# Splitting a weight tile in one pass of 1024 columns or in two of 512, on ScalarE and VectorE

## The chip, the core and the metric

The kernel runs on one core of a Trainium2 chip. The metric is the device time of one execution in microseconds (us); lower is better. Its engines are TensorE (PE in the profile; PEld is its weight load), VectorE (DVE), ScalarE (ACT), GpSimd (POOL) and SyncE (SP), which issues the weight transfers.

## What is computed

Two layers of a decoder trunk on 256 tokens of 1024 channels, all in float32. Cut to what matters here:

```python
def reference(x, ...):
    for l in range(2):
        h = rms_norm(x, norm_mix_g[l])
        mix = conv_sgu_mixer(h, ...) if l % 2 == 0 else moba_mixer(h, ...)
        x = x + mix
        h = rms_norm(x, norm_ffn_g[l])
        x = x + peer(h, peer_w_q[l], peer_subkeys[l], peer_u[l], peer_v[l])
    return rms_norm(x, norm_final_g)

def peer(h, w_q, subkeys, u_tab, v_tab):     # 128^2 one-neuron experts, 8 heads, 16 experts each
    q = (h @ w_q).reshape(T, 8, 2, 128)
    s = einsum('thpd,hpkd->thpk', q, subkeys)
    ...                                       # top 16 of each side, then top 16 of their sums
    act = gelu(einsum('td,thkd->thk', x, u_tab[expert]))
    return einsum('thk,thkd->td', softmax(sc) * act, v_tab[expert])
```

The kernel does not gather experts: it multiplies with the whole tables `u` and `v` (each 16384 x 1024) and uses gates that are zero where an expert was not picked.

## The kernel before

**Tiles and split.** All weights are streamed as 600 tiles of 128 partitions x 1024 columns: `w_in` 16, `w_out` 8, `q0` 16, `u0` 128, `v0` 128, `qkv` 24, `w_o` 8, `q1` 16, `u1` 128, `v1` 128 (table `STREAM`). SyncE loads each tile into one of 4 buffers `raw`. A float32 product is made of three matmuls in the type fp32r, so each tile is split into a high and a low part: ScalarE rounds it (`w_hi`, line 406), and VectorE subtracts the rounded value from the raw one (`w_lo`, line 603). The activations are split in the same way (`x_hi`, `x_lo`, or `ag_hi`, `ag_lo` for the table `v`). TensorE then runs 24 matmuls of 128x256 for each tile: 8 blocks `m` of 128 columns, times high by high, high by low, low by high (lines 1035 to 1037 in `project`, 1180 to 1182 in `combine`).

**Halves.** The split is made in halves of 512 columns. `w_hi` and `w_lo` have 4 buffers of one half each, which is two tiles. The semaphore `hi_ready` counts rounded halves, `split_ready` subtracted halves (TensorE waits for it ahead of each half, SyncE for the second half of the tile that is to be overwritten), `half_used` counts halves that TensorE has finished.

**Order.** There is no scheduler: the order on each engine is the order in which the code stands, and waits are on semaphores. All engines work two tiles ahead. On ScalarE (`taking`) one step is: wait until tile n is used, take its result out of PSUM (`take`), then round both halves of tile n+2 (`ahead`). For `w_out` and `w_o`, ScalarE only rounds (`only_ahead`), and VectorE takes the result (`add_residual`). On VectorE the two subtractions of tile n+2 stand between the other work of that step:

- in the `q` stages (`q_body`), between the pieces that rank the scores of the keys (`rank_keys`);
- in the first 8 turns of each `u` stage (`u_body`, a turn is 4 tiles), one half ahead of each of the 8 pieces of `pick` (maxima, places, comparison line 812, masks line 819, sums line 824). These are called pick turns below;
- in turns 9 to 16 of `u` (`late_body`), behind two `one_hots`, whose result TensorE scatters with 16 small matmuls for each tile (line 1147); in the remaining turns (`early_body`) behind one `one_hots` and ahead of `gate_late` and `apply_gates`;
- in the `v` stages (`v_body`), behind the subtraction that makes `ag_lo` (line 967).

The conv, gating and attention parts between the projections have no weight tiles.

Of the kernel before, what the change touches and what calls it, by code (L numbers as in the profile page):

```python
# [20 lines left out]
F32 = mybir.dt.float32  # L21
# [7 lines left out]
P = 128  # L29
# [39 lines left out]
SPLIT = 4  # L69
# [61 lines left out]
def build(nc, a, out):  # L131
    ctx = ExitStack()
    with ctx:
# [12 lines left out]
        w_hi = sb("w_hi", [P, SPLIT, HALF], F32R)  # L146
        w_lo = sb("w_lo", [P, SPLIT, HALF], F32R)
# [93 lines left out]
        half_used = sem("half_used")  # L241
# [157 lines left out]
        def _(act):  # L399
            def round_half(name, k, j, b):  # L400

                u = 2 * (TILE0[name] + 4 * k + j) + b
                act.wait_ge(loaded[j % RAW], loaded_count(name, k, j))
                at_least(act, half_used, u - SPLIT + 1)
                s = (2 * j + b) % SPLIT
                act.activation(w_hi[:, s, :], raw[:, j % RAW, b * HALF:(b + 1) * HALF], ACT.Copy).then_inc(hi_ready, 1)  # L406

            def ahead(name, k, j):

                if isinstance(k, int) and TILE0[name] + 4 * k + j + 2 >= TILES:  # L410
                    return
                for b in range(2):
                    round_half(name, k, j + 2, b)

            def taking(name, take, turns, k0=0, first=0, last=0, besides=None):

                def body(k):
                    for j in range(4):
                        act.wait_ge(half_used, 2 * (TILE0[name] + 4 * (k + k0) + j) + 2)
# [28 lines left out]
            for j in range(2):  # L448
                for b in range(2):
                    round_half("w_in", 0, j, b)  # L450
# [44 lines left out]
            def experts(l):  # L495
# [48 lines left out]
                def body(k):  # L544
                    for j in range(4):
                        act.wait_ge(half_used, 2 * (TILE0[act_v] + 4 * k + j) + 2)
                        round_ag(k, j)
                        ahead(act_v, k, j)
                sweep(act, NKEYS // 4, body, last=1)

            def taking_first(name, take):
                def body(k):
                    for j in range(4):
                        act.wait_ge(half_used, 2 * (TILE0[name] + 4 * k + j) + 2)
# [42 lines left out]
        def _(dve):  # L597
            def lower_half(name, k, j, b):

                u = 2 * (TILE0[name] + 4 * k + j) + b  # L600
                dve.wait_ge(hi_ready, u + 1)
                s = (2 * j + b) % SPLIT
                dve.tensor_tensor(w_lo[:, s, :], raw[:, j % RAW, b * HALF:(b + 1) * HALF], w_hi[:, s, :].bitcast(F32),  # L603
                                  ALU.subtract).then_inc(split_ready, 1)

            def ahead(name, k, j, last_wait=None):

                if isinstance(k, int) and TILE0[name] + 4 * k + j + 2 >= TILES:
                    return
                for b in range(2):  # L610
                    if b and last_wait:
                        dve.wait_ge(*last_wait)
                    lower_half(name, k, j + 2, b)
# [44 lines left out]
            for j in range(2):  # L658
                for b in range(2):
                    lower_half("w_in", 0, j, b)  # L660
# [28 lines left out]
            def add_residual(name):  # L689
                def body(k):  # L690
                    for j in range(4):
                        dve.wait_ge(half_used, 2 * (TILE0[name] + 4 * k + j) + 2)
# [192 lines left out]
            def experts(l):  # L885
# [5 lines left out]
                def q_body(k):  # L891
                    for j in range(4):
# [7 lines left out]
                        lower_half(q, k, j + 2, 0)  # L900
# [3 lines left out]
                        lower_half(q, k, j + 2, 1)  # L904
# [73 lines left out]
                dve.wait_ge(half_used, 2 * (TILE0[v] + NKEYS))  # L978
# [42 lines left out]
        def _(pe):  # L1021
            def project(name, k, j, operand=None):
# [4 lines left out]
                for b in range(2):  # L1027
                    pe.wait_ge(split_ready, 2 * n + b + 1)
                    s = (2 * j + b) % SPLIT
                    for i in range(4):  # L1030
                        m = 4 * b + i
                        if operand is not None and isinstance(k, int) and k == j == 0 and m % 2 == 0:
                            pe.wait_ge(operand_ready[operand], m // 2 + 1)
                        hi, lo = (w[:, s, i * P:(i + 1) * P] for w in (w_hi, w_lo))
                        pe.matmul(proj_ps[j % 2], hi, x_hi[:, m, :], start=(m == 0), stop=False)  # L1035
                        pe.matmul(proj_ps[j % 2], hi, x_lo[:, m, :], start=False, stop=False)  # L1036
                        mm = pe.matmul(proj_ps[j % 2], lo, x_hi[:, m, :], start=False, stop=(m == KD - 1))  # L1037
                    mm.then_inc(half_used, 1)
# [75 lines left out]
            def experts(l):  # L1114
# [53 lines left out]
                def combine(k):  # L1168
                    for j in range(4):
# [3 lines left out]
                        for b in range(2):  # L1173
                            pe.wait_ge(split_ready, 2 * n + b + 1)
                            s = (2 * j + b) % SPLIT
                            for c in range(4):
                                m = 4 * b + c
                                hi, lo = (w[:, s, c * P:(c + 1) * P] for w in (w_hi, w_lo))

                                pe.matmul(y_ps[:, m, :], hi, ag_hi[:, j % 2, :], start=begin and m % 2 == 0, stop=False, skip_group_check=True)  # L1180
                                pe.matmul(y_ps[:, m, :], hi, ag_lo[:, j % 2, :], start=False, stop=False, skip_group_check=True)  # L1181
                                mm = pe.matmul(y_ps[:, m, :], lo, ag_hi[:, j % 2, :], start=False, stop=end, skip_group_check=True)  # L1182
                            mm.then_inc(half_used, 1)
# [94 lines left out]
```

## Time and profile before

| | |
|---|---|
| device time, median of 3 runs | 2322.8 us (2320.18 to 2323.11) |
| span of the profiled execution | 2329.5 us (no other time is kept for it) |
| TensorE busy | 2168.4 us, 93% |
| TensorE weight load busy | 2090.0 us, 90% |
| VectorE busy | 1646.3 us, 71% |
| ScalarE busy | 1037.1 us, 45% |
| DMA | 323.57 MB, 139 GB/s over the span |

By start and end in the profiled execution, the stages of layer 0 lie about here: `w_in` 30 to 77 us, conv and gating to 162, `w_out` to 186, `q0` 196 to 271, pick turns of `u0` 274 to 389, turns 9 to 16 to 553, the rest of `u0` to 790, `v0` to 1163; then `qkv`, attention, `w_o`, and layer 1's `q1`, `u1`, `v1` in the same form. Busy times are averages over stages with different limits, so a stage is read by its own rows. The engines' busy times overlap and are not to be added. A busy TensorE is read by the distance between the starts of its matmuls, since each matmul is drawn longer than that distance.

### The profile page before, as it was taken

Reading aid. Unit: us, or ns where it says so; the run is one execution under the profiler, and the core shown is the slowest. Engines: PE = TensorE matmul, PEld = TensorE weight load, DVE = VectorE, ACT = ScalarE, POOL = GpSimd, SP = SyncE. Lnnn points to the kernel's source line nnn. Section 1 sums busy time; section 2 is a strip of 40 time slices with the busy share of each in tenths; the row PEclk is TensorE's granted clock in tenths of the full one; section 3 lists DMA queues with packets and bytes.
Section 4 is the critical chain, followed back from the end, with each engine's and each line's share of the span. In section 5 each row is a group of like instructions: output and inputs, shape, how many; then the busy total and the mean of one; then the engine's idle time right before and its main releaser. Section 6 shows DMA issues by size and latency. Waiting matters only on the chain.

```text
span 2329.5 us, 52851 instructions
## 1 busy us (share of the span) xinstructions
PE 2168.4 (93%) x17092; PEld 2090.0 (90%) x17092; DVE 1646.3 (71%) x3922; ACT 1037.1 (45%) x2162; POOL 19.8 (1%) x43
## 2 busy tenths in 40 slices
PE   6778798999999999999999987989999999999998
PEld 5558788999999999999987677889999999999998
DVE  3657998777888655555544589977788886555555
ACT  4334355444333355555544443544443333555554
POOL 1000000000000000000001000000000000000000
PEclk9779999999999899999998999999999998999999
DMA  5203344333443355555552233433334343555553
GB/s 179 73 23 115 115 162 140 106 107 126 138 141 137 116 180 180 183 185 181 182 184 95 71 111 117 162 128 108 108 128 143 136 143 119 183 184 180 180 182 125
DMA packets 90032, 323.57 MB, mean 139 GB/s; under 512 B 9914, under 2 KB 11994, under 8 KB 89728
## 3 DMA queue, kind: packets, MB, share of 16 engines
q1 hardware_dynamic: 88528, 316.71, 39.8%
q0 software_dynamic: 1456, 6.23, 0.8%
q8 instruction: 29, 0.48, 0.1%
q14 instruction: 19, 0.16, 0.0%
HBM read 321.82 MB, written 1.08 MB: 139 GB/s over the span
## 4 chain that ended last, share of the span: by engine, by line
PE 75%; DVE 12%; issue 9%; ACT 2%; DVEq 1%; DMA 0%; POOL 0%; ACTq 0%; POOLq 0%
PE psum L1180 11%; PE psum L1181 11%; PE psum L1182 11%; PE psum L1035 10%; PE psum L1036 9%; PE psum L1037 9%; PE psum L1147 9%; DVE w_lo L603 2%; DVE big L812 1%; ACT w_hi L406 1%; PE psum L1205 1%; DVE big L824 1%; PE psum L1208 1%; DVE big L819 1%; PE psum L1047 1%
## 5 line engine op out<-in xcount | busy, mean ns | idle before, releaser
L603 DVE TENSOR_TENSOR w_lo<-raw,w_hi 128x512 fp32r<-128x512 f32 x1200 | 781.8, 687 | 245.4 <-ACT w_hi L406 242.5
L1035 PE MATMUL psum<-x_hi,w_hi 128*128 128x256 f32 x2752 | 808.9, 294 | 77.9 <-DVE w_lo L603 44.5
L1036 PE MATMUL psum<-x_lo,w_hi 128*128 128x256 f32 x2752 | 785.3, 285 | 0.0
L1037 PE MATMUL psum<-x_hi,w_lo 128*128 128x256 f32 x2752 | 785.2, 285 | 0.0
L406 ACT ACTIVATE w_hi<-raw 128x512 fp32r<-128x512 f32 x1200 | 685.6, 619 | 39.4 <-PE psum L1037 28.8
L1035 PEld LDWEIGHTS psum<-x_hi,w_hi 128*128 128x128 f32 x2752 | 534.8, 194 | 91.1 <-DVE w_lo L603 57.1
L1180 PE MATMUL psum<-ag_hi,w_hi 128*128 128x256 f32 x2048 | 581.9, 284 | 2.9 <-DVE ag_lo L967 2.9
L1181 PE MATMUL psum<-ag_lo,w_hi 128*128 128x256 f32 x2048 | 581.5, 284 | 0.0
L1182 PE MATMUL psum<-ag_hi,w_lo 128*128 128x256 f32 x2048 | 581.4, 284 | 0.0
L1036 PEld LDWEIGHTS psum<-x_lo,w_hi 128*128 128x128 f32 x2752 | 535.5, 195 | 0.0
L1037 PEld LDWEIGHTS psum<-x_hi,w_lo 128*128 128x128 f32 x2752 | 534.1, 194 | 0.0
L1180 PEld LDWEIGHTS psum<-ag_hi,w_hi 128*128 128x128 f32 x2048 | 395.2, 193 | 3.3 <-DVE ag_lo L967 3.3
L1181 PEld LDWEIGHTS psum<-ag_lo,w_hi 128*128 128x128 f32 x2048 | 395.3, 193 | 0.0
L1182 PEld LDWEIGHTS psum<-ag_hi,w_lo 128*128 128x128 f32 x2048 | 395.3, 193 | 0.0
L967 DVE TENSOR_TENSOR ag_lo<-big,ag_hi 128x256 fp32r<-128x256 f32 x256 | 108.8, 425 | 307.2 <-ACT ag_hi L537 306.3
L1147 PE MATMUL psum<-hot_i,hot_j 128*128 128x68 f32 (+1 forms) x2048 | 262.7, 277 | 12.4 <-DVE big L876 5.4
L1147 PEld LDWEIGHTS psum<-hot_i,hot_j 128*128 128x128 f32 x2048 | 253.7, 197 | 18.8 <-DVE hot_i L870 10.6
L537 ACT ACTIVATE ag_hi<-big 128x256 fp32r (+1 forms) x252 | 105.2, 417 | 366.4 <-PE psum L1182 366.4
L867 DVE TENSOR_TENSOR hot_j<-const,picks 128x512 f32<-128x512 f32 x256 | 174.8, 683 | 0.0
L528 ACT ACTIVATE fresh<-psum 128x256 f32<-128x256 f32 x120 | 46.1, 384 | 279.8 <-PE psum L1037 279.8
L507 ACT ACTIVATE big<-psum 128x256 f32 x136 | 52.1, 383 | 209.7 <-PE psum L1037 209.3
L865 DVE TENSOR_TENSOR hot_i<-const,picks 128x240 f32<-128x240 f32 (+1 forms) x256 | 106.7, 417 | 1.4 <-PE psum L1147 0.7
(149 smaller groups left out, 1156.5 us busy)
## 6 DMA issues: line engine op xcount, KB each, us to landing
raw<-in_peer_u SPq DMA_DIRECT2D x256, 512.0 KB, 3.2
raw<-in_peer_v SPq DMA_DIRECT2D x256, 512.0 KB, 3.4
raw<-in_peer_q SPq DMA_DIRECT2D x32, 512.0 KB, 3.3
raw<-in_w_qkv SPq DMA_DIRECT2D x24, 512.0 KB, 3.2
raw<-in_w_in SPq DMA_DIRECT2D x16, 512.0 KB, 3.5
raw<-in_w_out SPq DMA_DIRECT2D x8, 512.0 KB, 3.3
raw<-in_w_o SPq DMA_DIRECT2D x8, 512.0 KB, 3.3
big<-bias_scratch POOLq DMA_DIRECT2D x1, 3072.0 KB, 12.1
```

The lines of the kernel that those rows point to most:

```text
L406: act.activation(w_hi[:, s, :], raw[:, j % RAW, b * HALF:(b + 1) * HALF], ACT.Copy).then_inc(hi_ready, 1)
L603: dve.tensor_tensor(w_lo[:, s, :], raw[:, j % RAW, b * HALF:(b + 1) * HALF], w_hi[:, s, :].bitcast(F32), ALU.subtract).then_inc(split_read ...
L865: dve.tensor_tensor(own_i, numbers[:, :, i0:i0 + rows].to_broadcast([P, 4, rows]), ahead_of[0].to_broadcast([P, 4, rows]), ALU.is_equal).t ...
L867: dve.tensor_tensor(own_j, numbers.to_broadcast([P, 4, P]), ahead_of[1].to_broadcast([P, 4, P]), ALU.is_equal).then_inc(hot_step, 1)
L967: dve.tensor_tensor(ag_lo[:, j % 2, :], big[:, bass.ds(i * T, T)], ag_hi[:, j % 2, :].bitcast(F32), ALU.subtract).then_inc(ag_ready, 1)
L1035: pe.matmul(proj_ps[j % 2], hi, x_hi[:, m, :], start=(m == 0), stop=False)
L1036: pe.matmul(proj_ps[j % 2], hi, x_lo[:, m, :], start=False, stop=False)
L1037: mm = pe.matmul(proj_ps[j % 2], lo, x_hi[:, m, :], start=False, stop=(m == KD - 1))
L1147: mm = pe.matmul(misc_ps[half][:, i * rows:(i + 1) * rows], hot_j[:, 4 * half + i, :], hot_i[:, 4 * half + i, 0:rows], start=True, stop=True)
L1180: pe.matmul(y_ps[:, m, :], hi, ag_hi[:, j % 2, :], start=begin and m % 2 == 0, stop=False, skip_group_check=True)
L1181: pe.matmul(y_ps[:, m, :], hi, ag_lo[:, j % 2, :], start=False, stop=False, skip_group_check=True)
L1182: mm = pe.matmul(y_ps[:, m, :], lo, ag_hi[:, j % 2, :], start=False, stop=end, skip_group_check=True)
```

## The change

Each tile is rounded by one ScalarE operation of 1024 columns and subtracted by one VectorE operation of 1024 columns. `w_hi` and `w_lo` have two buffers of a whole tile, so the memory is the same. `hi_ready`, `split_ready` and the renamed `tile_used` count tiles. TensorE waits once per tile, ahead of its first matmul. On VectorE, the subtraction stands where the first half stood (in `q_body` where the second stood), and the pieces that had a half between them follow each other.

```diff
-SPLIT = 4
+SPLIT = 2
...
-        w_hi = sb("w_hi", [P, SPLIT, HALF], F32R)
-        w_lo = sb("w_lo", [P, SPLIT, HALF], F32R)
+        w_hi = sb("w_hi", [P, SPLIT, D], F32R)
+        w_lo = sb("w_lo", [P, SPLIT, D], F32R)
...
-                    at_least(sp, split_ready, 2 * (TILE0[name] + 4 * k + j - RAW) + 2)
+                    at_least(sp, split_ready, TILE0[name] + 4 * k + j - RAW + 1)
...
-            def round_half(name, k, j, b):
-
-                u = 2 * (TILE0[name] + 4 * k + j) + b
+            def round_tile(name, k, j):
+
+                n = TILE0[name] + 4 * k + j
                 act.wait_ge(loaded[j % RAW], loaded_count(name, k, j))
-                at_least(act, half_used, u - SPLIT + 1)
-                s = (2 * j + b) % SPLIT
-                act.activation(w_hi[:, s, :], raw[:, j % RAW, b * HALF:(b + 1) * HALF], ACT.Copy).then_inc(hi_ready, 1)
+                at_least(act, tile_used, n - SPLIT + 1)
+                act.activation(w_hi[:, j % SPLIT, :], raw[:, j % RAW, :], ACT.Copy).then_inc(hi_ready, 1)
...
-            def lower_half(name, k, j, b):
-
-                u = 2 * (TILE0[name] + 4 * k + j) + b
-                dve.wait_ge(hi_ready, u + 1)
-                s = (2 * j + b) % SPLIT
-                dve.tensor_tensor(w_lo[:, s, :], raw[:, j % RAW, b * HALF:(b + 1) * HALF], w_hi[:, s, :].bitcast(F32),
+            def lower_tile(name, k, j):
+
+                dve.wait_ge(hi_ready, TILE0[name] + 4 * k + j + 1)
+                s = j % SPLIT
+                dve.tensor_tensor(w_lo[:, s, :], raw[:, j % RAW, :], w_hi[:, s, :].bitcast(F32),
                                   ALU.subtract).then_inc(split_ready, 1)
...
                         new[0]()
-                        lower_half(q, k, j + 2, 0)
                         if old:
                             old[3]()
                         dve.wait_ge(scores_copied, 16 * l + r + 1)
-                        lower_half(q, k, j + 2, 1)
+                        lower_tile(q, k, j + 2)
                         new[1]()
...
-                        lower_half(u, k, i // 2 + 2, i % 2)
+                        if i % 2 == 0:
+                            lower_tile(u, k, i // 2 + 2)
                         parts[i]()
...
-                for b in range(2):
-                    pe.wait_ge(split_ready, 2 * n + b + 1)
-                    s = (2 * j + b) % SPLIT
-                    for i in range(4):
-                        m = 4 * b + i
+                pe.wait_ge(split_ready, n + 1)
+                s = j % SPLIT
+                for m in range(KD):
...
-                    mm.then_inc(half_used, 1)
+                mm.then_inc(tile_used, 1)
```

Two places show what this does to the order. The first is VectorE in a pick turn, from the end of the piece `second_places` to the comparison (`big` holds all scratch tiles, `pick_step` is VectorE's own counter of these pieces). Before:

```order
L801 MAX_INDEX big<-big 128x8 x2
L769 ISA
L769 COPY big<-big 128x100
L601 ISA
L603 TENSOR_TENSOR w_lo<-raw,w_hi 128x512 [waits hi_ready]
L806 REGISTER_ALU
L807 CAST big<-big 128x2x8 [waits pick_step]
L601 REGISTER_ALU
L603 TENSOR_TENSOR w_lo<-raw,w_hi 128x512 [waits hi_ready]
L810 REGISTER_ALU
L812 TENSOR_TENSOR big<-big,const 128x800 [waits pick_step]
L812 TENSOR_TENSOR big<-big,const 128x800
```

With the change:

```order
L793 MAX_INDEX big<-big 128x8 x2
L761 ISA
L761 COPY big<-big 128x100
L597 REGISTER_ALU
L599 TENSOR_TENSOR w_lo<-raw,w_hi 128x1024 [waits hi_ready]
L798 REGISTER_ALU
L799 CAST big<-big 128x2x8 [waits pick_step]
L802 REGISTER_ALU
L804 TENSOR_TENSOR big<-big,const 128x800 [waits pick_step]
L804 TENSOR_TENSOR big<-big,const 128x800
```

The half that stood between the conversion (CAST) and the comparison is gone, so the comparison waits for the conversion directly in front of it. The other three tiles of a turn change in the same way.

The second place is VectorE in the loop of a `v` stage, one step of it and the start of the next. Before:

```order
L967 TENSOR_TENSOR ag_lo<-big,ag_hi 128x256
L601 ISA
L603 TENSOR_TENSOR w_lo<-raw,w_hi 128x512 [waits hi_ready]
L601 REGISTER_ALU
L603 TENSOR_TENSOR w_lo<-raw,w_hi 128x512 [waits hi_ready]
L966 REGISTER_ALU
L967 ISA [waits ag_hi_ready]
L967 TENSOR_TENSOR ag_lo<-big,ag_hi 128x256
```

With the change:

```order
L959 TENSOR_TENSOR ag_lo<-big,ag_hi 128x256
L597 REGISTER_ALU
L599 TENSOR_TENSOR w_lo<-raw,w_hi 128x1024 [waits hi_ready]
L958 REGISTER_ALU
L959 ISA [waits ag_hi_ready]
L959 TENSOR_TENSOR ag_lo<-big,ag_hi 128x256
```

Where the first of two subtractions could start behind the first rounded half, the one subtraction starts behind the whole rounded tile.

## Rows read from the trace of the kernel before

**Rows 1.** The page: its first line, and the chain that ended last by engine

```profile
span 2329.5 us, 52851 instructions
...
PE 75%; DVE 12%; issue 9%; ACT 2%; DVEq 1%; DMA 0%; POOL 0%; ACTq 0%; POOLq 0%
```

**Rows 2.** Windows, pick turns and v0: stretch, length, busy (instructions) PE PEld DVE ACT POOL, clock, DMA

```profile
290.00:389.00 99.00, 90.23 (x720) 87.19 (x720) 90.01 (x251) 52.41 (x100) 0.00 (x0) 1.00 0.48 162
...
800.00:1160.00 360.00, 360.00 (x3002) 360.00 (x3002) 212.70 (x376) 182.02 (x375) 0.00 (x0) 1.00 0.53 182
```

**Rows 3.** Groups of instructions: busy us, mean ns of one, then idle before

```profile
L603 DVE TENSOR_TENSOR w_lo<-raw,w_hi 128x512 fp32r<-128x512 f32 x1200 | 781.8, 687 | 245.4 <-ACT w_hi L406 242.5 <-DVE big L824 1.9 <-DVE big L769 0.2
L406 ACT ACTIVATE w_hi<-raw 128x512 fp32r<-128x512 f32 x1200 | 685.6, 619 | 39.4 <-PE psum L1037 28.8 <-DMA raw<-in_w_in 7.5 <-PE psum L1182 3.1
...
L460 ACT ACTIVATE big<-big 128x1024 f32<-128x1024 f32 x2 | 2.0, 1048 | 0.0
...
L649 DVE TENSOR_TENSOR big<-big 128x1024 f32<-128x1024 f32 x2 | 2.5, 1225 | 0.1
```

**Rows 4.** Timeline of v0, one step: start us, length us, engine, line

```profile
902.58 1.14 ACT L406 ACTIVATE w_hi<-raw 128x512 fp32r<-128x512 f32 x2
...
903.23 1.29 DVE L603 TENSOR_TENSOR w_lo<-raw,w_hi 128x512 fp32r<-128x512 f32 x2
...
904.83 0.28 PE L1180 MATMUL psum<-ag_hi,w_hi 128*128 128x256 f32 x1
...
905.14 0.42 ACT L537 ACTIVATE ag_hi<-big 128x256 fp32r x1 [1.42 <-PE psum L1182]
```

**Rows 5.** Timeline of VectorE, one pick turn of u0

```profile
316.06 0.69 DVE L603 TENSOR_TENSOR w_lo<-raw,w_hi 128x512 fp32r<-128x512 f32 x1 [0.16 <-DVE big L824]
...
321.03 0.69 DVE L603 TENSOR_TENSOR w_lo<-raw,w_hi 128x512 fp32r<-128x512 f32 x1 [0.59 <-ACT w_hi L406]
...
322.32 1.89 DVE L812 TENSOR_TENSOR big<-big,const 128x800 f32<-128x800 f32 x2
...
329.16 0.69 DVE L603 TENSOR_TENSOR w_lo<-raw,w_hi 128x512 fp32r<-128x512 f32 x1 [0.16 <-DVE big L824]
```

**Rows 6.** Timeline of ScalarE in the same turn

```profile
320.09 0.38 ACT L507 ACTIVATE big<-psum 128x256 f32 x1 [2.66 <-PE psum L1037]
320.37 1.14 ACT L406 ACTIVATE w_hi<-raw 128x512 fp32r<-128x512 f32 x2
```

**Rows 7.** Timeline of TensorE in the same turn, behind a wait

```profile
316.81 0.39 PE L1035 MATMUL psum<-x_hi,w_hi 128*128 128x256 f32 x1 [0.94 <-DVE w_lo L603]
317.03 0.28 PE L1036 MATMUL psum<-x_lo,w_hi 128*128 128x256 f32 x1
```

**Rows 8.** Timeline of turns 9 to 16 of u0, one tile: three engines

```profile
458.52 1.14 ACT L406 ACTIVATE w_hi<-raw 128x512 fp32r<-128x512 f32 x2
...
459.18 1.29 DVE L603 TENSOR_TENSOR w_lo<-raw,w_hi 128x512 fp32r<-128x512 f32 x2 [2.17 <-ACT w_hi L406]
...
461.77 2.34 PE L1147 MATMUL psum<-hot_i,hot_j 128*128 128x60 f32 x16 [0.28 <-DVE hot_i L870]
```

**Rows 9.** Timeline of VectorE in q0: the first half of two successive tiles

```profile
225.32 0.68 DVE L603 TENSOR_TENSOR w_lo<-raw,w_hi 128x512 fp32r<-128x512 f32 x1
...
229.50 0.68 DVE L603 TENSOR_TENSOR w_lo<-raw,w_hi 128x512 fp32r<-128x512 f32 x1
```

**Rows 10.** Timeline of w_in, one tile

```profile
50.86 1.29 DVE L603 TENSOR_TENSOR w_lo<-raw,w_hi 128x512 fp32r<-128x512 f32 x2 [1.59 <-ACT w_hi L406]
...
50.21 1.15 ACT L406 ACTIVATE w_hi<-raw 128x512 fp32r<-128x512 f32 x2
```

**Rows 11.** Timeline of VectorE, the first pick turn of u0

```profile
281.75 0.69 DVE L603 TENSOR_TENSOR w_lo<-raw,w_hi 128x512 fp32r<-128x512 f32 x1 [2.69 <-ACT w_hi L406]
```

**Rows 12.** Timelines of w_out (ScalarE) and of the last turns of u0 (VectorE)

```profile
167.97 0.63 ACT L406 ACTIVATE w_hi<-raw 128x512 fp32r<-128x512 f32 x1 [0.81 <-PE psum L1037]
...
607.34 1.29 DVE L603 TENSOR_TENSOR w_lo<-raw,w_hi 128x512 fp32r<-128x512 f32 x2 [0.56 <-ACT w_hi L406]
```

More of the change, by code:

```diff
@@ L240, in build @@
         split_ready = sem("split_ready")
-        half_used = sem("half_used")
+        tile_used = sem("tile_used")
         proj_taken = sem("proj_taken")
@@ L448, in _ @@
             for j in range(2):
-                for b in range(2):
-                    round_half("w_in", 0, j, b)
+                round_tile("w_in", 0, j)
             act.wait_ge(line_ps, 1)
@@ L597, in _, with ahead @@
         def _(dve):
-            def lower_half(name, k, j, b):
-                u = 2 * (TILE0[name] + 4 * k + j) + b
-                dve.wait_ge(hi_ready, u + 1)
-                s = (2 * j + b) % SPLIT
-                dve.tensor_tensor(w_lo[:, s, :], raw[:, j % RAW, b * HALF:(b + 1) * HALF], w_hi[:, s, :].bitcast(F32),
+            def lower_tile(name, k, j):
+                dve.wait_ge(hi_ready, TILE0[name] + 4 * k + j + 1)
+                s = j % SPLIT
+                dve.tensor_tensor(w_lo[:, s, :], raw[:, j % RAW, :], w_hi[:, s, :].bitcast(F32),
                                   ALU.subtract).then_inc(split_ready, 1)
-            def ahead(name, k, j, last_wait=None):
+            def ahead(name, k, j):
                 if isinstance(k, int) and TILE0[name] + 4 * k + j + 2 >= TILES:
                     return
[L610 to L613, printed above, removed]
+                lower_tile(name, k, j + 2)
             def norm(r, gain, s):
@@ L658, in _ @@
             for j in range(2):
-                for b in range(2):
-                    lower_half("w_in", 0, j, b)
+                lower_tile("w_in", 0, j)
             dve.wait_ge(params_in, 16 * PARAMS)
@@ L977, in experts @@
                 sweep(dve, NKEYS // 4, v_body, last=1)
-                dve.wait_ge(half_used, 2 * (TILE0[v] + NKEYS))
+                dve.wait_ge(tile_used, TILE0[v] + NKEYS)
                 for m in range(KD):
@@ L1026, in project @@
                 at_least(pe, proj_taken, p - 1)
-                for b in range(2):
-                    pe.wait_ge(split_ready, 2 * n + b + 1)
-                    s = (2 * j + b) % SPLIT
-                    for i in range(4):
-                        m = 4 * b + i
[L1032 to L1037, printed above, removed]
-                    mm.then_inc(half_used, 1)
+                pe.wait_ge(split_ready, n + 1)
+                s = j % SPLIT
+                for m in range(KD):
+                    if operand is not None and isinstance(k, int) and k == j == 0 and m % 2 == 0:
+                        pe.wait_ge(operand_ready[operand], m // 2 + 1)
+                    hi, lo = (w[:, s, m * P:(m + 1) * P] for w in (w_hi, w_lo))
+                    pe.matmul(proj_ps[j % 2], hi, x_hi[:, m, :], start=(m == 0), stop=False)
+                    pe.matmul(proj_ps[j % 2], hi, x_lo[:, m, :], start=False, stop=False)
+                    mm = pe.matmul(proj_ps[j % 2], lo, x_hi[:, m, :], start=False, stop=(m == KD - 1))
+                mm.then_inc(tile_used, 1)
             def projections(name, tiles, operand=None):
@@ L1172, in combine @@
                         begin, end = isinstance(i, int) and i == 0, isinstance(i, int) and i == NKEYS - 1
[L1173 to L1183, printed above, removed]
+                        pe.wait_ge(split_ready, n + 1)
+                        s = j % SPLIT
+                        for m in range(KD):
+                            hi, lo = (w[:, s, m * P:(m + 1) * P] for w in (w_hi, w_lo))
+                            pe.matmul(y_ps[:, m, :], hi, ag_hi[:, j % 2, :], start=begin and m % 2 == 0, stop=False, skip_group_check=True)
+                            pe.matmul(y_ps[:, m, :], hi, ag_lo[:, j % 2, :], start=False, stop=False, skip_group_check=True)
+                            mm = pe.matmul(y_ps[:, m, :], lo, ag_hi[:, j % 2, :], start=False, stop=end, skip_group_check=True)
+                        mm.then_inc(tile_used, 1)
                 sweep(pe, NKEYS // 4, combine, first=1, last=1)
```

10 lines of the change are left out of this document (5 added, 5 removed).

## The prediction

> **What bounds the kernel now.** I read the chain of waits first: TensorE holds 75% of it and VectorE 12% [rows 1], so most of the span is matmuls back to back, and VectorE sets the pace in a few stages. The windows say which. In a `v` stage TensorE is busy all of 360 us at full clock, with VectorE at 59% and ScalarE at 51% [rows 2]; one tile takes 2.88 us (ScalarE's step recurs at that distance, and the 24 matmuls start 0.12 apart). In the pick turns both engines are near their limit: TensorE 91%, VectorE 91% [rows 2], and a turn of 4 tiles takes 329.16 - 316.06 = 13.10 us [rows 5], against 4 x 2.88 = 11.52 of matmuls. In the `q` stages VectorE has no gap and a tile takes 229.50 - 225.32 = 4.18 us [rows 9].
>
> So what counts is not the busy time of the split but its **latency**: TensorE finishes tile n, ScalarE takes the result and rounds tile n+2, VectorE subtracts, and TensorE needs the result 2.88 us later, when tile n+1 is done. With halves this chain is a short pipeline: VectorE works on the first half while ScalarE rounds the second, and TensorE starts with the first. The change makes the three run one after the other.
>
> **Prices of the two new operations.** Two roundings of 512 last 1.14 us together [rows 4], 0.52 from start to start and 0.62 for the last. For one of 1024 the nearest row is another ScalarE operation of that shape: 1.05 us [rows 3]. From 0.62 for 512, with 0.42 for the 512 columns more, it would be 1.04; I take 1.04 (bounds 1.00 and 1.06). Two subtractions last 1.29 [rows 4], 0.60 and 0.69. One of 1024 is 1.225 by the nearest row [rows 3]; I take 1.22 (bounds 1.20 and 1.24), of which the next operation overlaps 0.08, as it does now (0.69 against 0.60). So VectorE saves 2 x 0.60 - 1.14 = 0.06 us for each tile, and ScalarE 0.10.
>
> ScalarE: Activation LUTs, in the section on what a table load costs, of the Trainium skill prices an operation without pointer operands at 186 ns + 0.833 ns per column, with 93 ns of overlap between neighbours. That gives 613 ns for 512 columns, which the rows bear out, and 1039 for 1024; by it the sum would be the same.
>
> **`v` stages (256 tiles).** Rounding starts at 902.58 [rows 4] and would end at 903.62. VectorE starts 0.04 behind it (in `w_in` the first rounded half, 50.21 + 0.61 = 50.82, is followed at 50.86 [rows 10]): 903.66 to 904.88. TensorE starts 0.06 behind a subtraction it waits for (316.06 + 0.69 = 316.75, then 316.81 [rows 5, 7]): 904.94. Now it starts that tile at 904.83 [rows 4], so it is 0.11 late; and behind a wait the second matmul follows at 0.22 instead of 0.12 [rows 7], another 0.10. This 0.21 comes back once for every two tiles, since the loop runs over tile n and n+2 (one loop for the even tiles, one for the odd, and the delay of one shifts the other): 0.105 us per tile, 256 x 0.105 = **+27**. Bounds: without the 0.10 it is 14; with the upper prices (0.04 more) 32.
>
> **`w_in`, `qkv`, and the last 4 plain tiles of each pick stage (48 tiles).** The same loop; only the taking in front is 0.28 instead of 0.32 long, so 0.17 per two tiles: 48 x 0.085 = **+4** (0 to 5). In `w_out` and `w_o` ScalarE rounds without taking anything: it could start at 167.97 [rows 12], the chain ends at 167.97 + 1.04 + 0.04 + 1.22 + 0.06 = 170.33, and that tile is due near 170.5 (one tile after its neighbour, which begins about 0.3 ahead of 167.97). I cost it at nothing; if the cover is gone, 16 tiles by 0.1 are 2 us.
>
> **Pick turns (8 per layer, 16).** The turn runs round a loop: first subtraction, TensorE's tile, ScalarE's taking and rounding, third subtraction, comparison, masks, sums, first subtraction of the next turn. Now the third subtraction starts 321.03 - 316.06 = 4.97 behind the first and has waited 0.59 for ScalarE [rows 5]. With the change: subtraction 1.22, TensorE 0.06, to the taking 320.09 - 316.81 = 3.28 [rows 6, 7], to the rounding 0.28, rounding 1.04, VectorE 0.04, which is 5.92; with TensorE's 0.10 behind a wait, 6.02. That is **+1.05**, and VectorE idles for some 1.5 us there, because its own pieces ahead are shorter by two halves. Then third subtraction to comparison: now 1.29 [rows 5]; after, 1.14 + 0.17 for the conversion + about 0.14 for the wait on it, which no filler covers any more (such a wait shows as 0.16 [rows 5]): 1.45, **+0.16**. From there to the next turn 6.84 [rows 5] loses 0.06. Sum +1.15 per turn, 16 turns: **+18** (without the bare wait and the 0.10: 14; with two more bare waits: 22). Each pick stage also ends with a tile that TensorE gets whole instead of by halves: 1.22 - 0.69 = 0.5, twice: **+1**.
>
> **Turns 9 to 16 of `u` (8 per layer).** Only one tile of each turn is tight: a table load of 1.28 us stands ahead of ScalarE's taking, and TensorE then waits 0.28 for `one_hots` [rows 8], which stand behind the subtraction on VectorE. The next operation there comes at 458.52 + 1.04 + 0.04 + 1.14 = 460.74 instead of 459.18 + 1.21 = 460.39: 0.35 later, and TensorE with it: 16 x 0.35 = **+6** (4 to 7). The other three tiles have no table load in the chain, 1.28 us more room; in the last turns of `u` VectorE sits idle 0.56 us per tile [rows 12], more than the 0.35: 0.
>
> **`q` stages.** VectorE is full, so 30 tiles by 0.06: **-2**. The copy of the scores is then followed by `second_values`, whose inputs are an operation older; I cost it at nothing (3 if each paid 0.1).
>
> SyncE's load into a raw buffer is released by the subtraction, 0.4 us later than now; the buffer is wanted again four tiles on, about 9 us, and the transfer takes 3.4: nothing. GpSimd has no part in this.
>
> **Sum**: 27 + 4 + 18 + 1 + 6 - 2 = +54 us. It is made against the profiled execution, whose span of 2329.5 [rows 1] lies 0.3% above the median of 2322.8; I put it on the median: 2377.
>
> **Rivals.**
>
> *The `v` loop is just not late.* The margin is 0.11 us in a chain of seven steps; if the subtraction took 1.11 or the rounding 0.93, all tiles outside the pick and late turns would be on time. Against it: both 1024-column rows. Time: 54 - 31 = +23, 2346.
>
> *The clock falls in the pick turns.* TensorE's wait at the head of a turn grows from 0.94 to about 2.1 us. In the first pick turn, which begins after 8.8 us of idle TensorE, VectorE waits 2.69 for ScalarE instead of 0.59 [rows 11], since the matmuls there run slower. If every turn paid these 2.1 us more: 16 x 2.1 = 34, 2411. Against it: the granted clock is 1.00 in these turns with gaps of 0.9 and 0.3 [rows 2, 7], and 2.1 is nearer to those than to 8.8.
>
> *Faster: fewer operations on a full engine.* The pick turns go by VectorE's work alone: it saves 4 x 0.06 per turn, and loses its 0.59 wait too, if the rounded tile is there when VectorE comes to the third subtraction. Then a turn takes 13.10 - 0.24 - 0.59 = 12.27, 16 turns save 13, the `q` stages 2, and the `v` loop holds: 2308. It decides whether ScalarE's rounding ends within 4.3 us (4.97 - 0.59 - 2 x 0.06) of the first subtraction's start; by my steps it ends at 6.0. For it speaks only the busy share of 91%; the 0.59 us wait on ScalarE speaks against. VectorE: DVE Perf Modes of the Trainium skill, rules for kernel authors, advises to keep the count of chained VectorE operations low rather than the count of semaphores; by that rule this rival would be the outcome, and the trace agrees with it only where VectorE never waits, in the `q` stages.
>
> That the change does not do what it says is excluded: the order shows one operation of 1024 on VectorE where two stood.
>
> **Chances.** Forecast (a loss in all three kinds of stage, 2358 to 2394 on its own) 0.77; `v` loop on time 0.09; clock 0.07; faster 0.05; all of it smaller than thought, within 0.2% (what a measurement of this kernel can tell from no change) 0.02. The range takes in the second case and the bounds: 2344 to 2398; outside are the clock and the two last cases. Faster 0.05, same 0.02, slower 0.93.
>
> **What would show it.** In `v`, TensorE should have a gap of about 0.1 us ahead of every tile or a double one ahead of every second, put down to the subtraction, and ScalarE's step should recur at 2.98 us. A pick turn should last 14.25 us, with about 1.5 us of waiting for ScalarE at the third subtraction. In turns 9 to 16 the wait of 0.28 should be 0.63. VectorE should be busy some 40 us less (600 tiles by 0.06). The prediction is wrong if the `v` stages keep 2.88 us a tile or the clock leaves 1.00.

## The result and the profile after

| | before | with the change |
|---|---|---|
| device time, median | 2322.95 us (2320.18 to 2324.05, 4 runs) | 2390.91 us (2385.75 to 2394.66, 4 runs) |
| span of the profiled execution | 2329.5 us | 2392.9 us (the run of 2394.66) |

The ratio is 1.0287, 95% interval 1.0262 to 1.0311: slower by 68 us. The forecast was 2377, with 2344 to 2398 as its range.

The page of the changed kernel, first line, busy lines and the chain that ended last, against [rows 1]:

```profile
span 2392.9 us, 49989 instructions
...
PE 2211.6 (92%) x17092; PEld 2110.7 (88%) x17092; DVE 1617.6 (68%) x3322; ACT 980.7 (41%) x1562; POOL 19.8 (1%) x43
...
PE 75%; DVE 11%; issue 10%; ACT 3%; DVEq 1%; DMA 0%; POOL 0%; ACTq 0%; POOLq 0%
```

VectorE worked 29 us less (some 40 were forecast) and ScalarE 56 us less, in 600 fewer operations each, and the kernel is 63 us longer by the spans. The page's groups of the two operations, against [rows 3]:

```profile
L599 DVE TENSOR_TENSOR w_lo<-raw,w_hi 128x1024 fp32r<-128x1024 f32 x600 | 734.5, 1224 | 407.9 <-ACT w_hi L405 405.0
...
L405 ACT ACTIVATE w_hi<-raw 128x1024 fp32r<-128x1024 f32 x600 | 628.8, 1048 | 44.6 <-PE psum L1027 33.6
```

One operation lasts 1.224 and 1.048 us, as forecast (1.22 and 1.04). What grew is VectorE's idle time ahead of the subtraction, nearly all of it waiting for ScalarE: 242.5 us before, 405.0 now.

Where the time went shows in the lengths of the stages, taken between the first starts of the operation that opens each (the scaling of `topi` for the pick stage, `picks`, the first `fresh`, the first `ag_hi`, the first addition of `y_ps`), in us:

| layer 0 / layer 1 | pick turns | turns 9 to 16 | rest of `u` | `v` |
|---|---|---|---|---|
| before | 123.1 / 122.7 | 160.0 / 161.1 | 234.5 / 234.4 | 374.2 / 371.6 |
| with the change | 133.4 / 134.4 | 168.4 / 166.5 | 235.1 / 235.1 | 386.9 / 383.8 |
| difference of both | +22.0 | +13.8 | +1.3 | +24.9 |

These make 62.0 of the 63.4 us.

One stretch changes its length from one run to the next, whatever the kernel, and has to be left out of comparisons: the attention of layer 1, from its first matmul with `anti` to the first addition of `w_o`. It took 69.3 us in the profile of before and 69.3 in that of the change, so these two compare fairly; in five of the eight experiments below it took 62. The window at its beginning, with the change (stretch, length, busy time of PE, PEld, DVE, ACT and POOL, each with its number of instructions, granted clock, DMA share, GB/s):

```profile
1285.00:1300.00 15.00, 14.74 (x31) 7.32 (x32) 4.21 (x10) 2.65 (x9) 2.23 (x7) 0.56 0.09 33
```

The same place in the profile of `act_whole`, a kernel of the next section:

```profile
1267.00:1282.00 15.00, 14.34 (x58) 7.92 (x58) 7.79 (x19) 5.41 (x19) 3.83 (x10) 1.00 0.09 33
```

So some 7 to 8 us between two runs of one kernel may be this alone. The unprofiled runs of before (2318 to 2324) have about the length that the short form would give: the profiled span of 2329.5 makes some 2331 of device time, if the 1.8 us between span and time of the change hold here too. That they have the short form was not seen. It may be one reason why the medians differ by 68 and the spans by 63.

The timeline of ScalarE and VectorE in `v0`, against [rows 4] (start us, length us):

```profile
940.47 0.42 ACT L534 ACTIVATE ag_hi<-big 128x256 fp32r x1 [1.52 <-PE psum L1170]
...
943.53 0.42 ACT L534 ACTIVATE ag_hi<-big 128x256 fp32r x1 [1.69 <-PE psum L1170]
943.85 1.04 ACT L405 ACTIVATE w_hi<-raw 128x1024 fp32r<-128x1024 f32 x1
...
944.93 1.23 DVE L599 TENSOR_TENSOR w_lo<-raw,w_hi 128x1024 fp32r<-128x1024 f32 x1 [0.42 <-ACT w_hi L405]
...
946.41 0.42 ACT L534 ACTIVATE ag_hi<-big 128x256 fp32r x1 [1.52 <-PE psum L1170]
```

The steps are 3.06 and 2.88 in turn: 5.94 for two tiles instead of 5.76. Rounding ends at 944.89, VectorE starts at 944.93 and ends at 946.16. TensorE's rows there:

```profile
946.00 0.28 PE L1170 MATMUL psum<-ag_hi,w_lo 128*128 128x256 f32 x1
946.21 0.38 PE L1168 MATMUL psum<-ag_hi,w_hi 128*128 128x256 f32 x1
946.43 0.28 PE L1169 MATMUL psum<-ag_lo,w_hi 128*128 128x256 f32 x1
```

It starts the tile 0.05 behind the end of the subtraction; the two distances of 0.21 and 0.22 replace two of 0.12, so the second matmul is 0.19 late. A stall this short hardly shows in the busy share, because the drawn end of one matmul covers it.

One pick turn on VectorE, against [rows 5]:

```profile
319.98 1.23 DVE L599 TENSOR_TENSOR w_lo<-raw,w_hi 128x1024 fp32r<-128x1024 f32 x1
...
325.89 1.23 DVE L599 TENSOR_TENSOR w_lo<-raw,w_hi 128x1024 fp32r<-128x1024 f32 x1 [1.16 <-ACT w_hi L405]
327.04 0.17 DVE L799 CAST big<-big 128x16 f32<-128x16 uint32 x1
327.24 1.90 DVE L804 TENSOR_TENSOR big<-big,const 128x800 f32<-128x800 f32 x2
...
334.00 1.23 DVE L599 TENSOR_TENSOR w_lo<-raw,w_hi 128x1024 fp32r<-128x1024 f32 x1
```

A turn is 14.02 us instead of 13.10. The third subtraction starts 5.91 behind the first (4.97 before) and has waited 1.16 for ScalarE (0.59 before). In layer 1 a turn at full clock takes 14.13: there the first subtraction starts 0.25 behind the end of the sums, in the turn above 0.13.

In turns 9 to 16, the tile behind the table load, TensorE's weight load, against [rows 8]:

```profile
476.57 0.97 PEld L1137 LDWEIGHTS psum<-hot_i,hot_j 128*128 128x128 f32 x8 [0.84 <-DVE hot_i L862]
...
496.47 0.97 PEld L1137 LDWEIGHTS psum<-hot_i,hot_j 128*128 128x128 f32 x8 [0.84 <-DVE hot_i L862]
```

A turn is 496.47 - 476.57 = 19.90 us against 19.52; the wait in front was 0.48 before in the same view. In TensorE's own rows, which the prediction had used, the wait went from 0.28 [rows 8] to 0.64, where it had said 0.63. But some turns are longer still. ScalarE's table load stands once in a turn:

```profile
358.47 1.28 ACT L504 ACT_TABLE_LOAD   x1 [1.68 <-PE psum L1027]
372.51 1.28 ACT L504 ACT_TABLE_LOAD   x1 [1.68 <-PE psum L1027]
387.77 1.28 ACT L504 ACT_TABLE_LOAD   x1 [1.52 <-PE psum L1027]
...
450.00 1.28 ACT L504 ACT_TABLE_LOAD   x1 [2.54 <-PE psum L1027]
471.40 1.28 ACT L504 ACT_TABLE_LOAD   x1 [2.54 <-PE psum L1027]
```

The pick turn from 372.51 took 15.26 us and not 14.02, the later turn from 450.00 took 21.40 and not 19.90. The windows of both show why; those of the first:

```profile
370.00:375.00 5.00, 4.98 (x41) 4.77 (x41) 5.00 (x7) 3.31 (x4) 0.00 (x0) 1.00 0.62 199
375.00:380.00 5.00, 3.28 (x23) 3.08 (x22) 4.90 (x20) 1.47 (x3) 0.00 (x0) 0.88 0.34 114
380.00:385.00 5.00, 5.00 (x36) 5.00 (x36) 2.37 (x9) 1.41 (x3) 0.00 (x0) 0.78 0.33 108
385.00:390.00 5.00, 5.00 (x43) 4.89 (x42) 5.00 (x6) 3.46 (x5) 0.00 (x0) 1.00 0.60 183
```

TensorE had started nothing for 2.0 us ahead of 377.26 (0.12 is the usual distance, so 1.9 were lost), and for part of the next stretch it was granted 1.2 and not 2.4 GHz. In the profile of before no turn shows such a fall. With the change there are three among the pick turns and five in turns 9 to 16, at 1.2 to 1.5 us each: some 11 us. I call such a stretch of 1.2 GHz inside a turn a fall of the clock.

### The profile page after: what moved, and what is told of

It is laid out like the page before. It is cut to its first block, busy times and chain, and to the rows that moved or that the text cites. A ratio compares the mean times of both kernels' runs of the same rounds, so it can differ in the third digit from the quotient of the medians.

```text
span 2392.9 us, 49989 instructions
## 1 busy us (share of the span) xinstructions
PE 2211.6 (92%) x17092; PEld 2110.7 (88%) x17092; DVE 1617.6 (68%) x3322; ACT 980.7 (41%) x1562; POOL 19.8 (1%) x43
## 4 chain that ended last, share of the span: by engine, by line
PE 75%; DVE 11%; issue 10%; ACT 3%; DVEq 1%; DMA 0%; POOL 0%; ACTq 0%; POOLq 0%
PE psum L1168 11%; PE psum L1169 10%; PE psum L1170 10%; PE psum L1025 10%; PE psum L1026 9%; PE psum L1027 9%; PE psum L1137 8%; DVE w_lo L599 2%; ACT w_hi L405 2%; PE psum L1193 1%; PE psum L1077 1%; DVE big L816 1%; PE psum L1196 1%; DVE big L811 1%; PE psum L1037 1%
## 5 line engine op out<-in xcount | busy, mean ns | idle before, releaser
L599 DVE TENSOR_TENSOR w_lo<-raw,w_hi 128x1024 fp32r<-128x1024 f32 x600 | 734.5, 1224 | 407.9 <-ACT w_hi L405 405.0
L1025 PE MATMUL psum<-x_hi,w_hi 128*128 128x256 f32 x2752 | 817.1, 297 | 90.9 <-DVE w_lo L599 58.6
L405 ACT ACTIVATE w_hi<-raw 128x1024 fp32r<-128x1024 f32 x600 | 628.8, 1048 | 44.6 <-PE psum L1027 33.6
L1168 PE MATMUL psum<-ag_hi,w_hi 128*128 128x256 f32 x2048 | 595.3, 291 | 2.9 <-DVE ag_lo L959 2.9
L1137 PEld LDWEIGHTS psum<-hot_i,hot_j 128*128 128x128 f32 x2048 | 252.9, 196 | 25.1 <-DVE hot_i L862 15.6
```

The source lines that it names most:

```text
L405: act.activation(w_hi[:, j % SPLIT, :], raw[:, j % RAW, :], ACT.Copy).then_inc(hi_ready, 1)
L599: dve.tensor_tensor(w_lo[:, s, :], raw[:, j % RAW, :], w_hi[:, s, :].bitcast(F32), ALU.subtract).then_inc(split_ready, 1)
L1137: mm = pe.matmul(misc_ps[half][:, i * rows:(i + 1) * rows], hot_j[:, 4 * half + i, :], hot_i[:, 4 * half + i, 0:rows], start=True, stop=True)
```

## The experiments

The kernels below, `ag_ahead` and `filler` excepted, are built on the kernel before, with halves or whole tiles chosen for each stage and engine. A whole operation then counts 2 on the semaphores of halves:

```diff
+            def round_whole(name, k, j):
+                n = TILE0[name] + 4 * k + j
+                act.wait_ge(loaded[j % RAW], loaded_count(name, k, j))
+                at_least(act, half_used, 2 * n - 2)
+                act.activation(w_hi[:, j % 2, :], raw[:, j % RAW, :], ACT.Copy).then_inc(hi_ready, 2)
...
+            def lower_whole(name, k, j):
+                dve.wait_ge(hi_ready, 2 * (TILE0[name] + 4 * k + j) + 2)
+                dve.tensor_tensor(w_lo[:, j % 2, :], raw[:, j % RAW, :], w_hi[:, j % 2, :].bitcast(F32),
+                                  ALU.subtract).then_inc(split_ready, 2)
```

The theory to test was latency: the chain of taking, rounding and subtracting must end within the time of one tile on TensorE. The main rival was that the long operations cost by themselves, the second that most of it is TensorE's clock.

**Whole tiles on ScalarE only** (`act_whole`).

```diff
+ROUND_WHOLE = ("w_in", "w_out", "q", "pick", "late", "early", "v", "qkv", "w_o")
+LOWER_WHOLE = ()
```

> ScalarE rounds whole tiles everywhere, VectorE still subtracts two halves. Latency theory: in v the first half is subtracted 904.35 on the clock of before, ahead of the 904.72 at which TensorE wants it, so v stays at 2.88 us a tile; a pick turn gets 0.42 longer (13.52, the first rounded half comes 0.42 later), the tight tile of turns 9 to 16 also 0.42 (19.94): 32 x 0.42 = 13, 2336 us. Rival: the length of each operation costs by itself, so that one half of the change costs about half of its 68 us: 2357, with v above 2.88.

Measured: 2353.6 us (2352.0 to 2354.0), ratio 1.014 (1.0124 to 1.0157). In `v`:

```profile
2031.69 0.42 ACT L552 ACTIVATE ag_hi<-big 128x256 fp32r x1 [1.51 <-PE psum L1223]
2032.01 1.04 ACT L416 ACTIVATE w_hi<-raw 128x1024 fp32r<-128x1024 f32 x1
2034.57 0.42 ACT L552 ACTIVATE ag_hi<-big 128x256 fp32r x1 [1.51 <-PE psum L1223]
...
2033.08 1.29 DVE L622 TENSOR_TENSOR w_lo<-raw,w_hi 128x512 fp32r<-128x512 f32 x2 [0.40 <-ACT w_hi L416]
```

The step is 2.88 us, and both `v` stages last as before (374.2 and 372.0): the same ScalarE operation as in the change costs nothing there, since the first half is subtracted in time. A pick turn takes the forecast 13.52, from the first subtraction of one to that of the next:

```profile
304.85 0.69 DVE L622 TENSOR_TENSOR w_lo<-raw,w_hi 128x512 fp32r<-128x512 f32 x1 [0.16 <-DVE big L854]
...
318.37 0.69 DVE L622 TENSOR_TENSOR w_lo<-raw,w_hi 128x512 fp32r<-128x512 f32 x1 [0.16 <-DVE big L854]
```

The total is 17 us above the 2336 expected. Turns 9 to 16 grew by 8.0 and 4.4 us instead of 3.4 each, with three falls of the clock in them; the rest of `u` grew by 2.6 for each layer, which the theory did not contain; the pick stages grew by 3.8 and 4.7 instead of 3.4. These make some 13 of the 17 us. What lengthened the rest of `u`, and the last 4 us, are open.

**Whole tiles on VectorE only** (`dve_whole`).

```diff
+ROUND_WHOLE = ()
+LOWER_WHOLE = ("w_in", "w_out", "q", "pick", "late", "early", "v", "qkv", "w_o")
```

> VectorE subtracts whole tiles everywhere, ScalarE still rounds two halves. Latency theory: the worst of all, since the subtraction now waits for the end of the two roundings, 0.10 us later than the one of 1024: a pair of v tiles takes 6.04, 3.02 a tile (+36), a pick turn 14.12 (+16), the tight tile of turns 9 to 16 +0.45 (+7), w_in and qkv +6, q -2: +63, and about 10 more if the clock falls as often as in the change: 2396 us. Rival, the ScalarE operation is what costs: then this is near before, 2323 to 2335; rival, both in equal shares: 2357.

Measured: 2441.5 us (2425.2 to 2443.5, 6 runs), ratio 1.0522 (1.0505 to 1.054). It is the worst of all, as of the stated theories only latency demanded, though ScalarE works in halves here. (By itself this run does not tell latency from a cost of VectorE's long operation; `ag_ahead` below does.) In `v`, ScalarE's steps are:

```profile
2030.61 0.42 ACT L552 ACTIVATE ag_hi<-big 128x256 fp32r x1 [1.41 <-PE psum L1223]
2030.94 1.14 ACT L409 ACTIVATE w_hi<-raw 128x512 fp32r<-128x512 f32 x2
2033.87 0.42 ACT L552 ACTIVATE ag_hi<-big 128x256 fp32r x1 [1.79 <-PE psum L1223]
...
2036.74 0.42 ACT L552 ACTIVATE ag_hi<-big 128x256 fp32r x1 [1.41 <-PE psum L1223]
```

Two tiles take 6.13 us (6.04 expected). The size was missed: +118 and not +74. The profile is of the shortest run (2425.2), and there `v` is 23.1 and 23.0 us longer than before, the pick turns 13.6 each, turns 9 to 16 7.7 and 6.1, the rest of `u` 5.3 and 5.2. Four of the six runs were 15 to 18 us longer, at a lower mean clock (0.957 against 0.965). The attention of layer 1, short in this profile, can be half of that; the rest no profile shows. The 5 us in the rest of `u`, where the theory had nothing, stay open too.

**Whole tiles in the `v` stages only** (`v_only`, and the same kernel again as `v_only_again`).

```diff
+ROUND_WHOLE = ("v",)
+LOWER_WHOLE = ("v",)
```

> Whole tiles (one rounding and one subtraction of 1024) in the two v stages alone, halves everywhere else. Latency theory: a v tile takes 2.97 us on average as in the change (steps of 3.06 and 2.88 in turn), all other stages as before: 256 x 0.09 = 23 us more than before, 2346 us (2343 to 2349). Rival, the clock: if the small gaps in v made TensorE's clock fall in v or behind it, 2355 or more. Rival, operation count: fewer operations make v no slower, 2323.

> The kernel with whole tiles in the v stages alone, once more, for a second profile: its four runs lay between 2357 and 2374 with a mean clock of 0.969 to 0.961, and the profiled one (2363) had no stretch in v below full clock. If this profile is of a longer run, some 5 us windows inside v or the pick turns show a clock under 1. Step of v: 3.02 us a tile as in the first profile.

Measured: 2368.5 us (2357.0 to 2374.3), ratio 1.0204 (1.0162 to 1.0245); again, in one run, 2363.4. Expected were 2346. The stages of `u` kept their lengths of before within 1.1 us, and `v` grew by 16.7 and 16.8 us in both profiles, not 12. Two tiles take 6.04 us instead of the change's 5.94. VectorE's row says where a part is:

```profile
2031.80 1.04 ACT L416 ACTIVATE w_hi<-raw 128x1024 fp32r<-128x1024 f32 x1
...
2032.94 1.22 DVE L628 TENSOR_TENSOR w_lo<-raw,w_hi 128x1024 fp32r<-128x1024 f32 x1 [0.48 <-ACT w_hi L416]
```

The subtraction starts 0.10 behind the end of the rounding, in the change 0.04. So this way of writing the semaphores adds its own delay, and in a chain without slack it counts in full. Both profiles hold the long form of the attention (70.3 us), so 7 to 8 us of the excess over 2346 are that, and 9 are the `v` stages. Neither has a fall of the clock in `v`; two of the unprofiled runs took 2374, and why is open. As a test of the size this kernel is blurred; that `v` alone is made slower by it, and that its gaps do not make the clock fall in a profiled run, it does show.

**Whole tiles in the pick turns only** (`pick_only`).

```diff
+ROUND_WHOLE = ("pick",)
+LOWER_WHOLE = ("pick",)
```

> Whole tiles in the pick turns alone (9 turns of each u stage on both engines). Latency theory: a pick turn takes 14.02 us at full clock against 13.10, 16 x 0.92 = 15, and 1 for the last tiles: 2339 us. Clock rival on top: in the change some pick turns took 15.3 and TensorE's granted clock fell there; if the gap of 2 us at the head of a turn is enough for that, 4 such turns add 5: 2344, and windows with a clock under 1 among the pick turns; turns 9 to 16 stay at 19.52. Operation count rival: 2319.

Measured: 2346.8 us (2344.3 to 2352.5), ratio 1.0115 (1.0093 to 1.0138). The pick stages last 134.4 and 135.3 us, 11.3 and 12.6 more than before, turns 9 to 16 and `v` stay within 1 us. One window of 5 us among the turns of layer 0 and two in layer 1 show a clock of 0.66. So the falls among the pick turns do not need those of the later turns; they come with the longer gap in the pick turns themselves. A turn at full clock takes 14.18 us here and not the 14.02 that were expected, so this way of writing the semaphores costs something here as well, 0.16 a turn.

**The change, with one step taken out of the chain in `v`** (`ag_ahead`). Both long operations stay. Only the order and the depth of the other pair are changed, with 4 buffers of `ag_hi` and `ag_lo` (for room, `rstd` lies in `fresh`, which is not in use at that time):

```diff
-                    i = 4 * k + j + 2
+                    i = 4 * k + j + 3
...
-                        round_ag(k, j)
                         ahead(act_v, k, j)
+                        round_ag(k, j)
...
-                        lower_ag(k, j)
                         ahead(v, k, j)
+                        lower_ag(k, j)
```

> The change as it is, but in the v stages ScalarE rounds the weight tile first and prepares ag_hi, ag_lo for three tiles ahead behind it (4 buffers of them), so that both 1024-column operations stay but 0.32 us leave the chain ahead of them. Latency theory: the chain ends 0.09 us before TensorE wants the tile, a v tile takes 2.88 again, 256 x 0.09 = 23 to 25 us are given back: 2366 us. Rival, the long operations cost v time by themselves (ports, power, clock): v stays at 2.97, 2391.

Measured: 2359.8 us (2358.1 to 2365.3), ratio to before 1.0167 (1.0152 to 1.0183). The `v` stages last 373.4 and 371.5 us, as before the change, with the 1024-column operations in them:

```profile
902.67 1.06 ACT L405 ACTIVATE w_hi<-raw 128x1024 fp32r<-128x1024 f32 x1 [1.58 <-PE psum L1170]
...
905.49 1.06 ACT L405 ACTIVATE w_hi<-raw 128x1024 fp32r<-128x1024 f32 x1 [1.46 <-PE psum L1170]
...
908.43 1.06 ACT L405 ACTIVATE w_hi<-raw 128x1024 fp32r<-128x1024 f32 x1 [1.58 <-PE psum L1170]
...
903.76 1.23 DVE L599 TENSOR_TENSOR w_lo<-raw,w_hi 128x1024 fp32r<-128x1024 f32 x1 [1.38 <-ACT w_hi L405]
```

Two tiles take 908.43 - 902.67 = 5.76. This settles the `v` stages: 0.32 us less in front of the same operations gives back all of their 25 us. The median is 31 us below that of the change and 6 below the 2366 expected; the profile has the short form of the attention, which can be those 6, and the pick stages (132.1 and 135.0) and turns 9 to 16 (166.0 and 166.6) are about as long as in the change.

**The change, with TensorE kept busy in its gaps** (`filler`).

```diff
+            def keep_busy(count):
+                for _ in range(count):
+                    pe.matmul(psum[:, 3, 0:T], x_hi[:, 0, 0:P], x_hi[:, 1, :], start=True, stop=True, skip_group_check=True)
...
+                        if j == 2:
+                            keep_busy(16)
                         project(name, k, j)
...
                         project(u, k, j)
+                        if j == 1:
+                            keep_busy(4)
```

> The change with matmuls into an unused PSUM bank where TensorE waits: 16 of them ahead of the third tile of each pick turn (some 1.9 of the 2.1 us), 4 ahead of the scatter behind the second tile in turns 9 to 16 (0.4 of 0.64). Clock theory: the turns of 15.3 (pick) and 21.4 us (9 to 16) go, since TensorE's clock no longer falls there; all are at 14.02 and 19.9, and 8 to 11 us are given back: 2381 us, clock 1.00 in those windows. Rival, the falls have nothing to do with the gaps (or the fillers delay the tiles): 2391 to 2400.

Measured: 2376.7 us (2375.9 to 2385.5), ratio to before 1.0231 (1.0215 to 1.0247), 14 us below the median of the change. But both kernels have runs of two lengths, 7 to 9 us apart, and not in the same proportion: the longest runs of the two differ by 9.2 us, the shortest by 9.9. The profile is of the longest run (2385.5; its attention in layer 1 took 69.3 us), and in it no turn of either kind shows a fall of the clock: turns 9 to 16 take 19.89 us, the pick turns 14.02 in layer 0 and 14.13 in layer 1. The same stretch as above:

```profile
375.00:380.00 5.00, 5.00 (x44) 4.99 (x43) 4.90 (x21) 1.45 (x3) 0.00 (x0) 1.00 0.35 113
380.00:385.00 5.00, 5.00 (x43) 4.89 (x42) 3.55 (x9) 2.66 (x4) 0.00 (x0) 1.00 0.47 137
```

Turns 9 to 16 last 163.5 and 164.0 us in all, 3.5 and 2.9 more than before, which is 8 x 0.37 = 3.0; the pick stage of layer 0 lasts 131.0, 7.9 more than before, which is 8 x 0.92 = 7.4 and the 0.5 at its end. Against the profile of the change the pick stages are 2.4 and 1.3 shorter, turns 9 to 16 4.9 and 2.5: the useless matmuls gained 11 us in these stages, of which 9 to 10 are left in the time of the whole kernel. In layer 1 the pick stage is still 10.4 longer than before. Of that, 2.1 lie ahead of its first table load, where the clock is low at the start of the stage (0.60, 0.50 and 0.87 in the 5 us windows from 1454.2 on; before 0.50, 0.74 and 1.00, from 1426.3 on); the same is so in the change.

**A version that beats both** (`fill_pick`). The kernel before waits 0.59 us per pick turn at the third subtraction [rows 5]. Half of the comparison can fill that:

```diff
-                        parts[i]()
+                        if i == 3:
+                            parts[3]()
+                            parts[4]()
+                            parts[5]([0])
+                        elif i == 5:
+                            parts[5]([1])
+                        elif i != 4:
+                            parts[i]()
...
+ROUND_WHOLE = ("q",)
+LOWER_WHOLE = ("q",)
```

> The kernel before with two edits: in the pick turns the first of the two comparisons stands ahead of the third tile's subtraction, where VectorE waits 0.59 us for ScalarE; in the q stages the subtraction is whole. Latency theory: a pick turn goes from 13.10 to 12.7 us, 16 x 0.4 = 6.6, and q gives 2: 2315 us. Rival, the delay of the third subtraction by 0.6 us moves TensorE's tile and the wait returns at the next turn: 2321 to 2324.

Measured: 2314.8 us (2314.4 to 2317.1, 6 runs), ratio 0.9968 (0.9956 to 0.998). A pick turn takes 12.90 us:

```profile
315.28 0.69 DVE L622 TENSOR_TENSOR w_lo<-raw,w_hi 128x512 fp32r<-128x512 f32 x1 [0.16 <-DVE big L855]
...
320.70 1.28 DVE L622 TENSOR_TENSOR w_lo<-raw,w_hi 128x512 fp32r<-128x512 f32 x2
321.90 0.98 DVE L843 TENSOR_TENSOR big<-big,const 128x800 f32<-128x800 f32 x1
323.13 0.69 DVE L622 TENSOR_TENSOR w_lo<-raw,w_hi 128x512 fp32r<-128x512 f32 x1 [0.24 <-ACT w_hi L409]
...
328.18 0.69 DVE L622 TENSOR_TENSOR w_lo<-raw,w_hi 128x512 fp32r<-128x512 f32 x1 [0.16 <-DVE big L855]
```

The wait at the third subtraction is gone, and 0.24 us of it come back at the fourth, so the turn gains 0.20, half of what was expected: 16 x 0.20 = 3.2, and the pick stages last 121.8 and 121.1 us against 123.1 and 122.7. The `q` stages gain 0.07 for each of 32 tiles, 2. That makes 5 of the 7.8 us between the medians. The two profiles differ by 16, of which 7.4 are the attention of layer 1 (61.9 against 69.3) and 2.9 the `qkv` stage of layer 1 (81.7 against 84.6), where the granted clock was low for a shorter time. The six runs of `fill_pick` lie within 3 us, those of before on the same chip between 2318.3 and 2323.9. So the gain is measured, its part of 5 us is explained, and whether the rest comes from the edit or from the clock in those stretches is open.

## Why the prediction was right

**The mechanism.** The prediction put the loss on the latency of the chain, against fewer operations on both engines. That VectorE saved busy time and the kernel lost 68 us is the result itself; `act_whole` (`v` unharmed, a pick turn at the forecast 13.52), `dve_whole` (worst) and `ag_ahead` (`v` restored with both long operations in it) show that it is the latency. In the pick turns and in turns 9 to 16 no experiment took the long subtraction out of the chain; there the cause rests on `act_whole` and on the rows.

**`v` stages, +27.** Measured +24.9. Late by 0.19 for two tiles, where the sum had 0.21; the shape is the one named (a double gap ahead of every second tile).

**Pick turns, +18 and +1.** At full clock a turn is 14.02 in layer 0 and 14.13 in layer 1, and not 14.25: 8 x 0.92 + 8 x 1.03 = 15.6. The two pieces in layer 0: the first to the third subtraction grew by 0.94 and not 1.05, because the sum counted the 0.10 behind a wait twice. The 3.28 from TensorE's start to ScalarE's taking had been read behind such a wait [rows 6, 7] and already held it; with the change the same distance is 3.27. The third subtraction to the comparison went from 1.29 to 1.35 and not to 1.45 (the wait behind the conversion, with nothing between, costs 0.03 and not 0.14). With 1 for the ends, 4 for three falls of the clock and 1 to 2 for the slower start in layer 1 the two stages grew by 22.0. VectorE's wait at the third subtraction is 1.16 and not 1.5; another 0.17 and 0.15 stand ahead of two of its smaller pieces before it.

**Turns 9 to 16, +6.** At full clock a turn grew by 0.37, which makes 5.9 for 16. Measured 13.8. This is the term that was mis-sized: the prediction looked for a fall of the clock only in the pick turns, where it gave it 34 us and 7%. It came in both kinds of turn, rarely, and cost 1.2 to 1.5 us each time (2.1 had been reckoned). So one of the prediction's own signs of being wrong, that the clock leaves 1.00, was met, though the time stayed in the range: the rival was right in kind and wrong in number, since not every turn pays. Of the 14 us between +54 and +68 about 11 are these falls. The other deviations are smaller and cancel in part: the slower start in layer 1 and the rest of `u`, which was put at 0, gave some 3 more than the sum, the full-clock pick turns and `v` 4 to 5 less, the medians 5 more than the spans. That the total came this near to the forecast is partly this cancelling. The sentence that held 1.00 against the rival had read a window of before, whose gaps were shorter.

**`w_in`, `qkv`, `q`.** The part that is left is small: two tiles of `w_in` take 5.90 us, as forecast (5.76 + 0.17), and a tile of `q` 4.11 instead of 4.18:

```profile
227.03 1.22 DVE L599 TENSOR_TENSOR w_lo<-raw,w_hi 128x1024 fp32r<-128x1024 f32 x1
...
231.14 1.21 DVE L599 TENSOR_TENSOR w_lo<-raw,w_hi 128x1024 fp32r<-128x1024 f32 x1
```

The `q` stage is the one place in which fewer, longer operations paid, because VectorE has no wait for ScalarE there. The rule of the Trainium skill that was cited for the faster rival (VectorE: DVE Perf Modes, rules for kernel authors: fewer operations rather than fewer semaphores) holds there, at 0.07 us a tile, and is outweighed in the kernel as a whole. The price that the Trainium skill gives for ScalarE's operation (ScalarE: Activation LUTs, what a table load costs), 1.039 us, stands beside a measured 1.048.

## What to carry to other kernels

Where a small operation stands between two uses of a double buffer, add up the chain from the release of a buffer to its being full again and compare it with the time of one tile; as long as it fits, the small operation costs nothing, and once it does not, the excess is paid once for every two tiles, and the busy shares show neither. Cutting an operation in two costs 0.06 to 0.10 us here and makes the stages overlap, so merge only where the engine never waits. Once TensorE's gaps grow, look at the granted clock of single turns and not of the whole stage, since a few rare falls can be a sixth of the loss.

## What the runs showed of the hardware that was not expected

- The granted clock can fall in one turn of a regular loop and not in the others, though the gaps look alike: with the change, in 3 of 16 pick turns (each turn has a gap of 1.9 to 2.1 us between matmuls) and in 5 of 16 later turns (0.84 and 0.27 us of idle weight load). Before, with 1.1 us in the pick turns and 0.48 and 0.27 in the later ones, there was none. With the change and 16 more matmuls in every pick turn and 4 in every later turn, no turn showed a fall, and these stages were 11 us shorter. Why one turn falls and its neighbour does not, no run here tells.
- The attention of layer 1 has one of two lengths, 62 us or 69 to 70, in kernels whose code is the same there (62 in five profiles, 69 to 70 in five); in the long form the granted clock is 0.56 at its start, in the short form 1.00. What decides which it is was not tried.
- The same wait of VectorE for ScalarE, from the end of the rounding to the start of the subtraction, took 0.04 us in the change and 0.10 in `v_only`, where only the instructions around it and the count it waits for are others. What makes the difference was not tried.
